# Decoder trunk, one core: a norm's moments kept in PSUM, and a stage's first half read input tile by input tile

## What is computed

```python
def _layernorm(x, g, b):
    mu = jnp.mean(xf, axis=-1, keepdims=True)
    var = jnp.mean(jnp.square(xf - mu), axis=-1, keepdims=True)
    return (xf - mu) * lax.rsqrt(var + LN_EPS) * g + b
def _swiglu(x, w_i, w_o):
    h = jnp.einsum('btd,df->btf', x, w_i)
    gate, up = h[..., :D_FF], h[..., D_FF:]
    return jnp.einsum('btf,fd->btd', jax.nn.silu(gate) * up, w_o)
y = _layernorm(ALPHA * y + 0.5 * _swiglu(y, ffn1_wi[l], ffn1_wo[l]), ...)
y = _layernorm(ALPHA * y + mixer(y), ...)
y = _layernorm(ALPHA * y + 0.5 * _swiglu(y, ffn2_wi[l], ffn2_wo[l]), ...)
```

## Time and profile before

| | us |
|---|---|
| median of 3 runs | 2185.98 |
| lowest, highest | 2183.97, 2189.35 |
| the profiled execution | 2186.89 |
| its span | 2185.1 |
| PE busy, share of the span | 2007.9, 92% |
| DVE, ACT, POOL busy | 856.9, 598.6, 513.3 |

### The profile page before, as it was taken

How to read it: one execution, slowest core, us unless ns; L and a number is a source line. 1 busy time by engine, 2 the same in 40 slices (tenths; PEclk the granted TensorE clock), 3 DMA queues, 4 the chain that set the end, 5 groups by cost and what they waited for, 6 DMA issues and landing times.

```text
span 2185.1 us, 36160 instructions
## 1 busy us (share of the span) xinstructions
PE 2007.9 (92%) x15485; PEld 1912.5 (88%) x15485; DVE 856.9 (39%) x1163; ACT 598.6 (27%) x837; POOL 513.3 (23%) x438
## 2 busy tenths in 40 slices
PE   5999999999897677999999999999998379999996
PEld 5999999976885457899999989999998379999996
DVE  2433322535836622543332254333224663333223
ACT  2221221422133242522122143212123452122123
POOL 2211121331400063511112132111121751111120
PEclk9999999988959868999999999999999689999998
DMA  5453322251100032233322322333221223332321
GB/s 169 135 173 96 89 83 99 69 145 39 42 1 1 5 94 78 58 96 96 96 83 83 105 78 77 96 96 93 82 101 33 59 60 96 96 88 85 101 74 40
DMA packets 258366, 179.55 MB, mean 82 GB/s; under 512 B 10806, under 2 KB 254782, under 8 KB 257757
## 3 DMA queue, kind: packets, MB, share of 16 engines
q1 hardware_dynamic: 250000, 154.90, 24.3%
q10 hardware_dynamic: 6165, 10.79, 1.8%
q0 software_dynamic: 2112, 12.59, 1.7%
HBM read 169.57 MB, written 8.08 MB: 81 GB/s over the span
## 4 chain that ended last, share of the span: by engine, by line
PE 81%; issue 6%; DVE 5%; ACT 3%; POOL 3%; DMA 1%; ACTq 0%; POOLq 0%; DVEq 0%
PE ps L797 69%; PE ps L896 3%; PE ps L840 2%; PE ps L901 1%; PE ps L998 1%; PE ps L914 1%; DVE xf L1247 1%; DVE xf L1253 1%; ACT w_hi L511 1%; DVE w_lo L1221 1%; PE ps L980 1%; POOL diag L1810 1%; PE ps L881 1%; POOL sum_sq L1734 1%; ACT xf L547 1%
## 5 line engine op out<-in xcount | busy, mean ns | idle before, releaser
L797 PE MATMUL ps<-xh,w_hi 128*128 128x260 f32 x3040 | 640.0, 286 | 39.5 <-ACT xh L542 17.8
L797 PE MATMUL ps<-xh,w_lo 128*128 128x260 f32 x3040 | 633.4, 284 | 0.0
L1221 DVE TENSOR_TENSOR w_lo<-w_raw,w_hi 128x2048 fp32r<-128x2048 f32 (+2 forms) x153 | 444.9, 2909 | 408.8 <-ACT w_hi L511 408.8
L797 PEld LDWEIGHTS ps<-xh,w_hi 128*128 128x128 f32 x3040 | 486.5, 191 | 45.1 <-issue 25.9
L797 PEld LDWEIGHTS ps<-xh,w_lo 128*128 128x128 f32 x3040 | 487.6, 191 | 0.2
L797 PE MATMUL ps<-xl,w_hi 128*128 128x260 f32 x3040 | 383.9, 283 | 1.3 <-POOL xl L1838 1.3
L797 PEld LDWEIGHTS ps<-xl,w_hi 128*128 128x128 f32 x3040 | 372.8, 189 | 1.7 <-POOL xl L1838 1.7
L511 ACT CAST w_hi<-w_raw 128x2048 fp32r<-128x2048 f32 (+2 forms) x153 | 281.9, 1843 | 283.2 <-PE ps L797 262.7
L797 PE MATMUL ps<-hh,w_hi 128*128 128x260 f32 x1408 | 292.9, 283 | 0.0
L797 PE MATMUL ps<-hh,w_lo 128*128 128x260 f32 x1408 | 291.4, 282 | 0.0
L1664 DVE TENSOR_TENSOR hid<-silu_g,ps 128x520 f32<-128x520 f32 x88 | 61.3, 696 | 548.5 <-ACT silu_g L710 514.7
(11 more groups left out here) (250 smaller groups left out, 1594.3 us busy)
## 6 DMA issues: line engine op xcount, KB each, us to landing
w_raw<-in_ffn_wi_dram SPq DMA_DIRECT2D x176, 512.0 KB
w_raw<-in_ffn_wo_dram SPq DMA_DIRECT2D x32, 1024.0 KB
w_raw<-in_ffn_wo_dram SPq DMA_DIRECT2D x16, 768.0 KB
w_raw<-in_attn_w_in_dram SPq DMA_DIRECT2D x8, 1024.0 KB
keys_scratch<-key_half POOLq DMA_DIRECT2D x2, 2048.0 KB, 7.9
w_raw<-in_attn_w_o_dram SPq DMA_DIRECT2D x4, 1024.0 KB
x_in<-in_x_prompt_dram ACTq DMA_DIRECT2D x1, 2048.0 KB
out_dram<-y_out ACTq DMA_DIRECT2D x4, 512.0 KB
```

Of the source, the lines that this page charges most:

```text
L797: mm = nc.tensor.matmul(ps[0:mc, bank + 2 * m + h, 0:HT], w[:, k, m, 0:mc], x(k)[:, h * HT:(h + 1) * HT], start=first and k == 0 and w is ...
L1221: nc.vector.tensor_tensor(w_lo[:, c % 2, 0:n], w_raw[:, c % 2, 0:n], w_hi[:, c % 2, 0:n].bitcast(F32), ALU.subtract).then_inc(s_lo, 1)
```

## The change

The moments stay in PSUM. `moment(q, h)` is bank 4h + 2q + 1 (mean in bank 1 or 5, mean square in 3 or 7), which are banks of half 1's products. `moments` loses its copy; the square of the mean goes to SBUF, the variance, its reciprocal and the root are written over the mean square in PSUM, and `normalise` reads both from PSUM.

A new function `first_half` takes half 0 of a stage's first two chunks: for each tile k the matmuls with `w_hi` and `w_lo` of the first chunk and with `w_hi` of the second, then `xl` of tile k-2 with the `w_hi` of both; the second chunk's `w_lo` comes last. Half 1's `stats` stands behind tile 2. On ACT `moments(1)` moves in front of the last three `affine` tiles of half 0 (of the last five in front of pl). Two transposes of pl and the write-out take other banks.

```diff
-        mean = hid[:, 0, :]
-        rstd = hid[:, 1, :]
+        mean_sq = hid[:, 1, :]
+        def moment(q, h):
+            return ps[:, 4 * h + 2 * q + 1, 0:HT]
...
                 act.wait_ge(s_stat, 2 * st.ln + h + 1)
-                nc.scalar.activation(mean[:, cols(h)], ps[:, h, 0:HT], ACT.Copy).then_inc(s_mean, 1)
-                nc.scalar.activation(rstd[:, cols(h)], ps[:, h, 0:HT], ACT.Square).then_inc(s_mean, 1)
+                nc.scalar.activation(mean_sq[:, cols(h)], moment(0, h), ACT.Square).then_inc(s_mean, 1)
...
-                nc.scalar.activation(rstd[:, cols(h)], rstd[:, cols(h)], ACT.Sqrt).then_inc(s_rstd, 1)
+                nc.scalar.activation(moment(1, h), moment(1, h), ACT.Sqrt).then_inc(s_rstd, 1)
...
-                affine(n, st, 0, split, order, windows, ahead, KD)
+                affine(n, st, 0, split, order, windows, ahead, ahead + 3)
                 moments(st, 1)
+                affine(n, st, 0, split, order, windows, ahead + 3, KD)
                 root(st, 1)
...
+            def first_half(st, middle):
+                def tile(j, w, x, k, start, stop):
+                    for m in range(2):
+                        nc.tensor.matmul(ps[:, 4 * j + 2 * m, 0:HT], w[j][:, k, m, :], x[:, k, cols(0)], start=start, stop=stop)
+                pe.wait_ge(s_lo, st.chunk + 3)
+                pe.wait_ge(s_free, 2 * (st.group + 1) + 2)
+                for k in range(KD + 2):
+                    if k < KD:
+                        pe.wait_ge(s_xh, first_x(st, 0) + k + 1)
+                        tile(0, wh, xh, k, k == 0, False)
+                        tile(0, wl, xh, k, False, False)
+                        if k == 0:
+                            pe.wait_ge(s_hi, st.chunk + 2)
+                        tile(1, wh, xh, k, k == 0, False)
+                    if k == 2 and middle is not None:
+                        middle()
+                    if k >= 2:
+                        pe.wait_ge(s_x, first_x(st, 0) + k - 1)
+                        tile(0, wh, xl, k - 2, False, k == KD + 1)
+                        tile(1, wh, xl, k - 2, False, False)
+                pe.wait_ge(s_lo, st.chunk + 4)
+                for k in range(KD):
+                    tile(1, wl, xh, k, False, k == KD - 1)
...
-                dve.wait_ge(s_mean, 4 * st.ln + 2 * h + 2)
-                v = rstd[:, cols(h)]
-                n = step(nc.vector.scalar_tensor_tensor(v, ps[:, 2 + h, 0:HT], eps, v, ALU.add, ALU.subtract))
+                dve.wait_ge(s_mean, 2 * st.ln + h + 1)
+                v = moment(1, h)
+                n = step(nc.vector.scalar_tensor_tensor(v, v, eps, mean_sq[:, cols(h)], ALU.add, ALU.subtract))
...
-                        n.append(step(nc.vector.tensor_tensor(x, x, mean[:, cols(h)], ALU.subtract)))
+                        n.append(step(nc.vector.tensor_tensor(x, x, moment(0, h), ALU.subtract)))
...
-                        nc.vector.tensor_tensor(x, x, rstd[:, cols(h)], ALU.mult).then_inc(s_t, 1)
+                        nc.vector.tensor_tensor(x, x, moment(1, h), ALU.mult).then_inc(s_t, 1)
```

More of the change, by code:

```diff
@@ L691, in poolmix @@
                     nc.scalar.activation(state_t[:, 4 * q:4 * q + 4].rearrange("p d b r -> p d (b r)"),
-                                         ps[:, q, :].rearrange("p (d n) -> p d n", d=4)[:, :, 0:DEC * PBUF],
+                                         ps[:, 6 * q, :].rearrange("p (d n) -> p d n", d=4)[:, :, 0:DEC * PBUF],
                                          ACT.Copy).then_inc(s_ste, 1)
@@ L762, in _ @@
                     act.wait_ge(s_tr, KD + 1 + 2 * i + q + 1)
-                    nc.scalar.activation(y_out[0:rows, i % 2, q * 512:(q + 1) * 512], ps[0:rows, 4 + 2 * (i % 2) + q, :],
+                    nc.scalar.activation(y_out[0:rows, i % 2, q * 512:(q + 1) * 512], ps[0:rows, 2 * (i % 2) + q, :],
                                          ACT.Copy).then_inc(s_ev, 1)
@@ L807, in first_x @@
                 return 0 if st.x == KD else st.x - 2 * KD + KD * h
-            def two_chunks(st, middle_0, middle_1):
[L811 to L819, removed]
+            def first_half(st, middle):
+                view = "p (k u c) -> p k u c"
+                wh = [w_hi[:, (st.chunk + j) % 2, :].rearrange(view, k=KD, u=2) for j in range(2)]
+                wl = [w_lo[:, (st.chunk + j) % 2, :].rearrange(view, k=KD, u=2) for j in range(2)]
+                def tile(j, w, x, k, start, stop):
[20 more added lines that the diff above has]
+                    tile(1, wl, xh, k, False, k == KD - 1)
@@ new lines, in two_chunks @@
+            def two_chunks(st, middle_0, middle_1):
+                first_half(st, middle_0)
+                for j in range(2):
+                    products(st.chunk + j, KD, 4 * j, x_hi, x_lo, True, True,
+                             before_hi=(lambda k: pe.wait_ge(s_xh, first_x(st, 1) + k + 1)) if j == 0 else None,
+                             before_lo=(lambda k: pe.wait_ge(s_x, first_x(st, 1) + k + 1)) if j == 0 else None,
+                             middle=middle_1 if j == 1 else None, only=(1,))
@@ L832, in stats @@
                     for n, x in enumerate(parts):
-                        if n >= 1 and q == 0:
-                            if h == 0:
-                                pe.wait_ge(s_last, 2 * st.ln + n)
-                            else:
-                                pe.wait_ge(s_free, first_free + 6 + n)
+                        if h == 1 and q == 0 and n <= 1:
+                            pe.wait_ge(s_free, first_free + 7 + n)
+                        elif n >= 1 and q == 0:
+                            pe.wait_ge(s_last if h == 0 else s_free, (2 * st.ln if h == 0 else first_free + 6) + n)
                         if n >= 1 and q == 1:
                             pe.wait_ge(s_sq, SQUARES * st.ln + 6 + 2 * h + n)
-                        mm = nc.tensor.matmul(ps[:, 2 * q + h, 0:HT], mean_ones, x[:, cols(h)], start=n == 0, stop=n == 2)
+                        mm = nc.tensor.matmul(moment(q, h), mean_ones, x[:, cols(h)], start=n == 0, stop=n == 2)
                 mm.then_inc(s_stat, 1)
@@ L1151, in poolmix @@
                     for d in range(4):
-                        mm = nc.tensor.transpose(ps[:, q, d * P:d * P + DEC * PBUF],
+                        mm = nc.tensor.transpose(ps[:, 6 * q, d * P:d * P + DEC * PBUF],
                                                  state_in[:, (4 * q + d) * P:(4 * q + d + 1) * P],
@@ L1200, in _ @@
                     for d in range(4):
-                        mm = nc.tensor.transpose(ps[0:rows, 4 + 2 * (i % 2) + q, d * P:(d + 1) * P],
+                        mm = nc.tensor.transpose(ps[0:rows, 2 * (i % 2) + q, d * P:(d + 1) * P],
                                                  xf[:, 4 * q + d, i * P:i * P + rows], ident)
```

## The result

| us | before | changed |
|---|---|---|
| median beside the change (5 runs each) | 2185.46 | 2168.47 |
| lowest, highest | 2183.97, 2189.35 | 2166.00, 2174.33 |
| ratio, 95% interval | | 0.9924, 0.9904 to 0.9944 |
| span of the profiled execution | 2185.1 | 2164.2 |

A forecast was written before the change was run, and what follows sets the result against it. PE was taken as the bound (81% of the chain), with gains only where stages meet: 1.54 + 1.69 + 0.15 + 2.98 + 1.2 = 7.56 us, from 2186.89 to 2179.3, as a median 2178.4 us; 8-in-10 range 2172 to 2184.

The forecast's parts named there:

- The tail between f2 and pl: Between f2 and pl, ACT starts half 1 sooner with the square moved ahead: 2.98 us, bounds 0 and 2.98.
- Behind f3: After the last network, the square is ready 1.35 us sooner, less 0.13 for the instruction in PSUM: 1.2 us.
- The copy: At pl to f3, half 0: ACT's copy saves 0.29 us, less 0.13 for `tensor_scalar` in PSUM; net 0.15 us.
- Half 1's waits: PE's waits for tiles 6 and 7 of half 1 go at the four boundaries: 1.69 us.
- PSUM as an operand: DVE's 192 `normalise` instructions: no cost taken; the rival had 65 ns each, 3.1 us, 2181.5 us, chance 0.11.
- the collision: Rival: DVE and PE collide in PSUM, 47 instructions on the path costing 26 us, so 2204 us; chance 0.05.
- half 0, tile by tile: At the four boundaries, PE does two more matmuls in each gap before tiles 1 and 2: 1.54 us.
- from tile 2 on PE was behind ACT's tiles, not ahead: In half 0 at the boundaries: ten matmuls a tile instead of four meet no wait, so most of the order gains nothing.
- I assume that the half clock ends at the same time as before: At f0 to pr, gap-filling counts half, 0.29 us instead of 0.58; pl to f3 repeats it.
- the half clock is shortened or spared: Rival at the boundaries: half clock lasts 3.4 us, each boundary wins 1.7 us more, 2171.6 us; chance 0.15.

The follow-up runs named there:

- square_not_moved: The changed kernel with the square of half 1's mean back behind all eight tiles of half 0; 2180.75 us, ratio 0.9968.
- before_filled: The kernel before with PE's pause ahead of tile 0 filled by 6 throw-away matmuls at the four boundaries; 2184.90 us, ratio 0.9983.
- moments_in_psum: The kernel before with only the moments put in PSUM and ACT's copy gone; 2185.67 us, ratio 0.9987.
- tile_by_tile: The kernel before with only half 0's order changed, tile by tile over both chunks; 2183.47 us, ratio 0.9969.
- pause_filled_less: The changed kernel with PE's pause before tile 0 filled by throw-away matmuls (6, and 13 at pl to f3); 2168.98 us, ratio 0.9916.
- units_filled: pause_filled_less with 2 and 8 more throw-away matmuls in PE's two pauses in the index units; 2158.11 us, ratio 0.9871.
- all_filled: units_filled with 10 instead of 13 matmuls in the pause between pl and f3; 2154.73 us, ratio 0.9851.

## Why the prediction was wrong

**What held.** The tail between f2 and pl: forecast 2.98, measured 12.16 - 9.06 = 3.10, and `square_not_moved` gives it back. Behind f3: 1.2 and 1.4; DVE goes from the last `normalise` to the variance without a pause. The copy: from the end of `stats(0)` at pl to tile 0 PE idles 6.04 us instead of 6.20, 0.16 for the forecast 0.15. Half 1's waits: 1.35 for 1.69. PSUM as an operand: 0.413 to 0.419 us in three profiles beside 0.421 in SBUF, so no cost in `normalise`; that rival falls, and so does the collision (26 us, slower), since no instruction of `normalise` exceeds 0.426 us. By this, the rule of the Trainium skill ("VectorE: DVE Perf Modes", the section on the errata) that I had weighed is not seen in the 192 instructions; `tensor_scalar` is the one that lengthened, from 0.296 to 0.44 us.

**The step that failed: half 0, tile by tile, 1.54 us, and that the terms were taken as independent.** From tile 0 to the end of `stats` the four boundaries took 34.1 and 32.7 us in the two executions of before, and 28.7, 24.1 and 29.3 in the changed kernel, with 8 matmuls more in them (0.96 us at full clock). That is 33.4 - 27.4 + 1.0 = 7.0 us, 5.5 more than the term, and it is most of what was missed. Two sentences of the step were wrong. One was "from tile 2 on PE was behind ACT's tiles, not ahead". It was read at half clock, where PE needs 0.87 us for a tile's four matmuls and ACT 0.99; there the waits are short and lie partly in the record of a tile's first matmul (0.55 instead of 0.42 us). `before_filled` shows the same place at full clock: waits at tiles 1 to 4, 1.5 us. With ten or six matmuls a tile instead of four one wait of 0.63 us is left of them. The other was "I assume that the half clock ends at the same time as before". It followed from the one execution that I had; within the four boundaries the old order had 26.7, 23.7 and (moments_in_psum) 26.0 us of half clock, the new order 20.0, 6.4 and 20.3, and 15.9, 13.5 and 10.4 in the three kernels that have the order and lack a part. That the order shortens it is likely by these nine profiles; why, they don't show.

The two sentences belong together. At half clock PE in the old order only filled its waits, so that the half clock cost it little: 29.5 us at op to f1 without it and 31.4 with 6.8 us of it, where the changed kernel takes 27.2 and 30.1. The change gains 2.3 us there at full clock and 1.3 at half clock, near the 1.0 forecast for that boundary. I had priced the case in which it gains least, and taken it for the only one.

The 7.0 us are what is won at this place with all three parts in the kernel. By itself the order keeps less: 3.3 us in `tile_by_tile`, still twice the term. The prediction added its terms as if each were worth the same with or without the others. In these kernels a PE that is ahead in half 0 waits in half 1, unless the moments in PSUM and the earlier square bring these tiles sooner.

Two readings were off as well. The half clock of the earlier trace rows lasts from 1294.8 to 1301.6 us and not from 1295.2 to 1302.0. With the fall at 1294.8, and at 902.2 at op to f1, most of the gap before tile 2 lies at half clock, and I had priced it at full clock.

**The rival "the half clock is shortened or spared"** named the right thing and stood at 0.15. Its price (1.7 us for each 3.4) was too high for the old order and its cause was incomplete: it gave the clock a gain on top of 7.56, while the gain of the order at full clock was missing.

**What was not in the sum.** Pl itself, 0.95 us: one collision fewer between DVE's small sums and POOL. And the comparison of two single executions: 20.9 us, of which 7.2 (5.1 in the index units, 2.1 in the attention) were chance of the kind that moves the same kernel by 5 and 9 us.

**Sum.** 6.1 (half 0, without the matmuls moved into it) + 2.3 (behind it, with them) + 3.1 + 0.1 (from `stats(0)` to tile 0, by the means) + 0.95 + 1.4 = 14.0 us of the profiles' means. The medians of the three sessions say 17.0, 16.4 and 20.0. The rest, 3 to 4 us by their mean, is not located. It goes with the granted clock (0.946 against 0.941 on the mean of all executions), but with two and three profiles of index units and attention, whose executions differ by up to 9 us, it can be chance or an effect of when these stages begin.

## What to carry to other kernels

A wait that a trace does not show may be hidden by a half clock: where PE's clock is low in the only profile, price the stage at both clocks, from the pace of the engine that feeds PE. Take the order that leaves PE most work per arriving tile, and try to fill PE's short pauses ahead of long work with throw-away matmuls that end before the awaited tile: here 28 or 31 of them at the four boundaries left no half clock there, and 10 in the index units brought 7 to 12 us. Don't add up the terms of parts that feed the same engine without asking what each is worth when the others are there. Judge such a change by cuts at fixed instructions in several profiles, since stretches that come and go move a span by more than the change.

## What was unexpected in the hardware

- A pause of 2.64 us, with full clock before it, was followed by half clock for 3.4 or 6.8 us in 13 of 15 cases (the first three boundaries in the five profiles of the two kernels); with the pause filled there was none in any of the twelve boundaries of pause_filled_less, units_filled and all_filled. The pause before tile 0 isn't all of it: in before_filled the old order had 3.4 us at f1 to f2 with that pause filled. Two pauses of 0.96 and 4.1 us in the index units went with 17 to 27 us of it, and with none when they were filled.
- DVE and POOL block each other when DVE's instruction has two operands in SBUF: 0.97 instead of 0.42 us on DVE, 5.95 instead of 0.75 on POOL. With one operand moved to PSUM both are gone, and what is left on POOL (2.5 us) coincides with DVE's `split_lo`, which has two SBUF operands. The Trainium skill says so ("SBUF — State Buffer", "SBUF: two separate sides"): a DVE operation with two SBUF inputs and a POOL operation that reads SBUF exclude each other for the whole instruction. The trace agrees: in the changed kernel 101 of the 192 instructions of `normalise` run beside one of POOL, and none takes over 0.426 us. Before, POOL's 5.95 us span ten instructions of `normalise` and a `split_lo` that follow each other without a pause.
- A matmul of float32 operands of 260 columns runs as two records and takes 0.42 to 0.44 us at full clock, 3.6 times one of the products (0.12 us), which are made from split operands.
